# Starting the expert sum with a written-out first scatter instead of clearing its banks

## The chip, the cores and the metric

The kernel runs on one core of one Trainium2 chip, in float32. The metric is the device time of one execution in microseconds (us); lower is better.

## What is computed

The reference is two transformer blocks one after the other on 256 tokens of width 1024, with two layers each. Every layer is a token mixer followed by a hierarchical mixture of experts (MoE). The mixers are not touched by the change; the MoE is. Cut to what matters:

```python
def hier_moe(h, wg, bg, we, be, w1, w3, w2):
    ...
    g_sel = jnp.argmax(g_logits, axis=-1)                  # one group of 4
    top_l, top_i = lax.top_k(e_logits, TOP_K_EXPERTS)      # two of its 8 experts
    gates = g_gate[:, None] * jax.nn.softmax(top_l, axis=-1)
    ...
    def expert_block(args):
        xi, e = args
        hid = jax.nn.silu(xi @ w1[e]) * (xi @ w3[e])
        return hid @ w2[e]

    yb = lax.map(expert_block, (xb, blk_exp)).reshape(p_rows, d)
    y = jnp.zeros((t, d), h.dtype).at[buf_tok].add(yb * buf_w[:, None].astype(yb.dtype))
```

So `y`, 256 tokens by 1024, is a sum over 32 experts: each expert's results are scattered to its tokens, multiplied by the gate. The first block has experts of inner width 512, the second of 256. There are four such MoEs, called MoE 0 to MoE 3 here (`m` in the code; 0 and 1 have kind 1, 2 and 3 have kind 2).

## The kernel before, in words

Five engines run programs of their own, tied by counting semaphores. Each engine waits for a value that its `Engine` helper counts along (`q.due(name)`), and the producer raises it (`then_inc`). TensorE (PE) multiplies, VectorE (DVE) and ScalarE (ACT) read the products out of PSUM, SyncE (SP) starts all weight transfers. The order of the work on each engine is written out by hand; no scheduler changes it.

Weights come through a ring of `NR = 6` slots of 2048 KB. SP fills a slot as soon as PE has finished the product that used its old content (`unit_done`), so it runs at most six slots ahead of PE and no further. In an MoE of kind 1 a pair of experts takes all six slots, in one of kind 2 three.

PSUM has 8 banks of 128x512 float32. `y` takes banks 4 to 7, two of its eight 128x256 chunks in each bank. Since all scatters add into it over the whole MoE, `before` begins by clearing the four banks: `pe_clear` (L1859) multiplies a tile of zeros into a bank with `start=True`. At what points of the start of an MoE each bank is cleared is set by the table `CLEARS`, because the banks come free at different times: `at_once`, `turned` (when ScalarE has read the tokens that were turned into those banks), `ranked` (behind the products of the ranks) and `last` (behind the gather).

The start of an MoE runs so, with the lines as in the profile:

1. PE turns the router's logits (L632). DVE picks group and experts out of them in a row of small operations (`dve_route`, L1754 to L1789) and raises `route_done`. Meanwhile ScalarE turns the tokens into the tile `xN` (L678) and raises `tokens_ready`.
2. PE, meanwhile: the clears `at_once`, in MoE 2 and 3 also the rows of scales (L2260), three products that only keep it at work (`pe_warm`, L2246), the wait for `tokens_ready`, the clears `turned`, then `pe_ranks` (L1746, L1748, L1749), whose first product waits for `route_done`, then the clears `ranked`.
3. DVE makes the ranks (L1795), copies the counts (L1797) and compares ranks with slots (L1799, twice, `place_ready`). Then it works out where each expert's tokens start (L1802 to L1819), which later steps need.
4. PE gathers the tokens of the first pair of experts (`pe_gather`, L400), with the clears `last` behind it. ScalarE (L1970) and DVE (L1977) scale what was gathered (`xg_ready`).
5. `pe_experts`: pairs of experts. A pair (`pe_pair`) is the products up (L1924, in kind 2 L1932), half of the scatter of the pair before (L1908), the turn of the hidden tile (L1945), the other half of that scatter, the products down (L1956) and the turn of the gates (L1962). The first pair has no scatter and sorts the tokens instead. In kind 1 the first pair is written out and 15 more run in a hardware loop (`Fori`); in kind 2 two pairs are written out and 7 passes of two pairs run in the loop.

Of the kernel before, what the change touches and what calls it, by code (L numbers as in the profile page):

```python
# [19 lines left out]
P = 128  # L20
D = 1024
KD = D // P
# [194 lines left out]
def build(nc, a, vec_at, vec_w, dense_at, out):  # L217

    ctx = ExitStack()
    with ctx:  # L220
# [33 lines left out]
        def v(name, *dims):  # L254
            at, n = vec_at[name]
            return view(VEC + at, *(dims or (n,)))
# [23 lines left out]
        mm = nc.tensor.matmul  # L280
# [1471 lines left out]
        def dve_route(q, m, rbank):  # L1752
# [41 lines left out]
            q.e.wait_ge(sems["ranks_ready"], q.due("ranks_ready"))  # L1794
            V.tensor_tensor(rank, psum[:, rbank, 128:192].rearrange("p (t e) -> p t e", t=NT), chosen, ALU.mult).then_inc(sems["dve_step"], 1)  # L1795
            q.e.wait_ge(sems["dve_step"], q.due("dve_step"))
            V.tensor_copy(counts, psum[:, rbank, 192:224])  # L1797
            for t in range(NT):
                ins = V.tensor_tensor(place[:, t], along(rank[:, t, 0:2], CAP), over(v("slots"), 2), ALU.is_equal)  # L1799
            ins.then_inc(sems["place_ready"], 1)  # L1800
            q.e.wait_ge(sems["place_ready"], q.due("place_ready"))
            V.tensor_reduce(most, counts, AX.X, ALU.max)  # L1802
            V.tensor_tensor_scan(starts_f, ones[:, 0:E], counts, 0.0, ALU.mult, ALU.add).then_inc(sems["dve_step"], 1)
            q.e.wait_ge(sems["dve_step"], q.due("dve_step"))
# [48 lines left out]

        y = banks(4, 4, KD, S)

        def pe_clear(which):

            for b in which:
                mm(psum[:, b, :], v("zeros"), v("causal"), start=True, stop=False, skip_group_check=True)  # L1859


        def pe_gather(q):

            for k in range(KD):
# [37 lines left out]
            q.e.wait_ge(sems["sorted_even"], q.due("sorted_even", KD // 2))  # L1902
            q.e.wait_ge(sems["sorted_odd"], q.due("sorted_odd", KD // 2))

        def pe_scatter(q, first, last):

            for c in range(first, last):
                ins = mm(y[:, c, :], ysl[:, P * c:P * c + P], gatedT, start=False, stop=False, skip_group_check=True)  # L1908
            return ins

        def pe_pair(q, kind, first, sort):

            if not first:
                q.e.wait_ge(sems["xg_ready"], q.due("xg_ready", 2))
            if kind == 1:
                for n in range(2):
                    for part in range(2):
                        w = slot(q)
                        if n == 1 and part == 0 and not first:
                            q.e.wait_ge(sems["gatedT_ready"], q.due("gatedT_ready"))  # L1920
                        for i in range(KD // 2):
                            k = part * (KD // 2) + i
                            for e in range(2):
                                ins = mm(psum[CAP * e:CAP * e + CAP, n, :], xg[:, k, CAP * e:CAP * e + CAP],  # L1924
                                         sl(w, KD)[:, e * (KD // 2) + i, :], start=(k == 0), stop=(k == KD - 1),
                                         skip_group_check=True)
                        ins.then_inc(sems["unit_done"], 1)
            else:
                w = [slot(q), slot(q)]
                for k in range(KD):  # L1930
                    for e in range(2):
                        ins = mm(psum[CAP * e:CAP * e + CAP, 0, :], xg[:, k, CAP * e:CAP * e + CAP], sl(w[e], KD)[:, k, :],  # L1932
                                 start=(k == 0), stop=(k == KD - 1), skip_group_check=True)
                ins.then_inc(sems["unit_done"], 1)
                if not first:
                    q.e.wait_ge(sems["gatedT_ready"], q.due("gatedT_ready"))
            if not first:
                q.e.wait_ge(sems["results_ready"], q.due("results_ready", 2))
                pe_scatter(q, 0, KD // 2)
            if sort:  # L1940
                pe_sort(q)
            fc = 4 if kind == 1 else 2
            q.e.wait_ge(sems["hid_ready"], q.due("hid_ready"))
            for f in range(fc):
                ins = nc.tensor.transpose(psum[:, 0, P * f:P * f + P], hid[:, P * f:P * f + P], ident)  # L1945
            ins.then_inc(sems["hid_turned"], 1)
            if not first:
                pe_scatter(q, KD // 2, KD)
            q.e.wait_ge(sems["hidT_ready"], q.due("hidT_ready"))
            for half in range(2):  # L1950
                if kind == 1 or half == 0:
                    down = slot(q)
                for f in range(fc):
                    for e in range(2):
                        w = sl(down, KD)[:, 4 * e + f, :] if kind == 1 else sl(down, 4)[:, 2 * e + f, 512 * half:512 * half + 512]
                        ins = mm(psum[CAP * e:CAP * e + CAP, 2 + half, :], hidT[:, f, CAP * e:CAP * e + CAP], w,  # L1956
                                 start=(f == 0), stop=(f == fc - 1), skip_group_check=True)
                if kind == 1 or half == 1:
                    ins.then_inc(sems["unit_done"], 1)
            q.e.wait_ge(sems["gated_ready"], q.due("gated_ready"))  # L1960
            for t in range(NT):
                ins = nc.tensor.transpose(psum[:, 1, P * t:P * t + P], gated[:, t].rearrange("p a b -> p (a b)"), ident)  # L1962
            ins.then_inc(sems["gated_turned"], 1)
# [65 lines left out]
        def pe_experts(q, kind, passes):  # L2029
            n = PAIRS[kind]  # L2030
            per = {f"slot{(q.slot + j) % NR}": 16 for j in range(NR)}
            per.update(gatedT_ready=n, results_ready=2 * n, hid_ready=n, hidT_ready=n, xg_ready=2 * n, gated_ready=n)
            for g in range(n):
                pe_pair(q, kind, g == 0, g == 0)
            with nc.tensor.Fori(1, passes) as i:
                q.enter(i, per, 1)
                for g in range(n):
                    pe_pair(q, kind, False, False)
                q.leave(passes - 1)

        SUM_TURN = (0, 1, 2, 3)

# [202 lines left out]
            for _ in range(n):  # L2245
                mm(psum[:, bank, :], ident, view(VEC + vec_at["cum64"][0], 512), start=True, stop=True, skip_group_check=True)  # L2246

        CLEARS = (((6,), (4, 5), (), (7,)), ((5,), (6, 7), (), (4,)), ((), (4, 5), (6, 7), ()))

        def pe_moe(q, m, src, kind, rbank):  # L2250
            at_once, turned, ranked, last = CLEARS[min(m, 2)]
            if m < 2:
                q.skip("scale_ready")
            pe_clear(at_once)
            if m >= 2:
                q.e.wait_ge(sems["scale_ready"], q.due("scale_ready"))
                for n in range(2):
                    for t in range(NT):
                        col = spread[:, t, 0:1] if n == 0 else invs[:, t:t + 1]
                        ins = mm(psum[:, 1, S * n + P * t:S * n + P * t + P], col.broadcast_to([P, P]), ident, start=True, stop=True)  # L2260
                ins.then_inc(sems["rows_ready"], 1)
            pe_warm((1, 1, 3)[min(m, 2)], 3)
            q.e.wait_ge(sems["tokens_ready"], q.due("tokens_ready"))
            pe_clear(turned)
            pe_ranks(q, rbank)
            pe_clear(ranked)
            q.e.wait_ge(sems["place_ready"], q.due("place_ready"))
            pe_gather(q)
            pe_clear(last)
            q.e.wait_ge(sems["xg_ready"], q.due("xg_ready", 2))  # L2270
            pe_experts(q, kind, PASSES[kind])
            q.e.wait_ge(sems["starts_ready"], q.due("starts_ready"))
# [665 lines left out]
```

## Time and profile before

| | |
|---|---|
| Median of 3 runs | 2630.02 us (2628.97 to 2632.25) |
| The profiled execution | 2625.74 us |
| Its span on the core | 2624.1 us |
| TensorE busy | 2446.5 us, 93% of the span, 11516 matrix products |
| VectorE busy | 670.6 us, 26% |
| ScalarE busy | 449.8 us, 17% |
| HBM traffic | 769.56 MB, 293 GB/s over the span |
| Clears (L1859) | 32 records of 0.592 us (median) |
| Share of the chain that ended last | PE 70%, DMA 24%, DVE 3%, ACT 2% |

A float32 product shows as two records of TensorE, so `x2` in a row of the trace is one instruction of the program. Records of successive products overlap a little, since each holds its pipeline's latency; the distance from start to start tells what a product costs in a row of products. MoE 0 lies at 323 to 805 us, MoE 1 at 970 to 1457, MoE 2 at 1757 to 2030, MoE 3 at 2340 to 2615.

### The profile page before, as it was taken

Reading aid. Unit: us, or ns where it says so; the run is one execution under the profiler, and the core shown is the slowest. Engines: PE = TensorE matmul, PEld = TensorE weight load, DVE = VectorE, ACT = ScalarE, POOL = GpSimd, SP = SyncE. Lnnn points to the kernel's source line nnn. Section 1 sums busy time; section 2 is a strip of 40 time slices with the busy share of each in tenths; the row PEclk is TensorE's granted clock in tenths of the full one; section 3 lists DMA queues with packets and bytes.
Section 4 is the critical chain, followed back from the end, with each engine's and each line's share of the span. In section 5 each row is a group of like instructions: output and inputs, shape, how many; then the busy total and the mean of one; then the engine's idle time right before and its main releaser. Section 6 shows DMA issues by size and latency. Waiting matters only on the chain.

```text
span 2624.1 us, 28427 instructions
## 1 busy us (share of the span) xinstructions
PE 2446.5 (93%) x11516; PEld 1402.3 (53%) x11516; DVE 670.6 (26%) x1400; ACT 449.8 (17%) x814; POOL 0.2 (0%) x4
## 2 busy tenths in 40 slices
PE   7999999888889999988888998999999998999998
PEld 4775743333336673333333777874444777874443
DVE  2653321111003231101001532143112434042113
ACT  3141110000002121010000133011111242112111
POOL 0000000000000000000000000000000000000000
PEclk9999999999999999999999999999999999999999
DMA  9348669999997137999999542147999232148994
GB/s 401 131 183 366 253 275 428 429 428 429 428 428 289 66 129 330 429 428 429 429 428 429 208 147 106 67 192 281 428 423 376 97 129 97 64 193 333 427 421 179
DMA packets 53936, 769.56 MB, mean 293 GB/s; under 512 B 5984, under 2 KB 6496, under 8 KB 7008
## 3 DMA queue, kind: packets, MB, share of 16 engines
q1 hardware_dynamic: 53568, 768.17, 70.9%
q8 instruction: 57, 0.93, 0.1%
q10 hardware_dynamic: 288, 0.26, 0.0%
q14 instruction: 23, 0.19, 0.0%
HBM read 767.36 MB, written 1.05 MB: 293 GB/s over the span
## 4 chain that ended last, share of the span: by engine, by line
PE 70%; DMA 24%; DVE 3%; ACT 2%; issue 1%; SPq 0%; ACTq 0%; DVEq 0%
DMA slab<-in_experts 23%; PE psum L400 14%; PE psum L432 13%; PE psum L1932 9%; PE psum L1924 8%; PE psum L1956 7%; PE psum L1908 5%; PE psum L696 4%; PE psum L503 1%; DMA slab<-in_dense 1%; PE psum L1240 1%; PE psum L626 1%; PE psum L1962 1%; PE psum L1859 0%; PE psum L1945 0%
## 5 line engine op out<-in xcount | busy, mean ns | idle before, releaser
L1924 PE MATMUL psum<-slab 128*64 128x512 f32 x2048 | 462.0, 597 | 78.1 <-DMA slab<-in_experts 76.7
L400 PE MATMUL psum<-slab 128*128 128x256 f32 (+6 forms) x1560 | 388.3, 405 | 10.7 <-ACT slab L2443 7.0
L432 PE MATMUL psum<-slab 128*128 128x256 f32 x1504 | 343.3, 389 | 11.8 <-DVE slab L2733 6.6
L1956 PE MATMUL psum<-slab 128*64 128x512 f32 x1536 | 343.7, 597 | 2.6 <-ACT slab L1992 2.6
L1924 PEld LDWEIGHTS psum<-slab 128*64 128x64 f32 x2048 | 138.5, 137 | 380.1 <-issue 264.2
L400 PEld LDWEIGHTS psum<-slab 128*128 128x128 f32 (+2 forms) x1560 | 272.8, 188 | 120.3 <-issue 71.4
L432 PEld LDWEIGHTS psum<-slab 128*128 128x128 f32 x1504 | 292.9, 196 | 60.0 <-issue 8.8
L1908 PE MATMUL psum<-slab 128*128 128x256 f32 x1024 | 249.7, 385 | 3.0 <-DVE slab L2016 3.0
L1932 PE MATMUL psum<-slab 128*64 128x512 f32 x1024 | 226.8, 596 | 3.1 <-DVE slab L1977 3.1
L1908 PEld LDWEIGHTS psum<-slab 128*128 128x128 f32 x1024 | 183.3, 189 | 73.1 <-issue 48.7
L2004 DVE TENSOR_TENSOR slab<-psum,slab 128x512 f32<-128x512 f32 (+1 forms) x64 | 35.7, 558 | 707.6 <-PE psum L1924 509.5
L1956 PEld LDWEIGHTS psum<-slab 128*64 128x64 f32 x1536 | 104.7, 137 | 206.2 <-issue 202.6
L2014 DVE COPY slab<-psum 128x512 f32<-128x512 f32 x64 | 44.2, 691 | 427.8 <-PE psum L1956 427.8
L1932 PEld LDWEIGHTS psum<-slab 128*64 128x64 f32 x1024 | 70.7, 137 | 136.3 <-issue 132.9
L1988 ACT ACTIVATE slab<-psum 128x512 f32<-128x512 f32 (+1 forms) x64 | 31.4, 490 | 555.3 <-PE psum L1924 345.7
L696 PE MATMUL psum<-slab 128*128 128x256 f32 x512 | 114.8, 381 | 0.0
L696 PEld LDWEIGHTS psum<-slab 128*128 128x128 f32 x512 | 96.0, 190 | 16.9 <-issue 3.7
L1992 ACT ACTIVATE slab<-psum 128x512 f32<-128x512 f32 (+1 forms) x64 | 31.4, 490 | 389.7 <-PE psum L1945 389.7
L1996 ACT ACTIVATE slab<-psum 128x512 f32<-128x512 f32 x64 | 38.2, 597 | 251.8 <-PE psum L1956 251.8
L447 ACT ACTIVATE slab<-psum 128x512 f32<-128x512 f32 (+3 forms) x45 | 25.4, 565 | 244.1 <-PE psum L432 174.1
L2731 DVE TENSOR_TENSOR slab<-psum,slab 128x1024 f32<-128x1024 f32 x16 | 19.6, 1224 | 178.6 <-PE psum L400 178.6
L503 PE MATMUL psum<-slab 128*32 128x512 f32 x384 | 47.2, 615 | 7.3 <-DMA slab<-in_dense 4.9
(431 smaller groups left out, 1563.3 us busy)
## 6 DMA issues: line engine op xcount, KB each, us to landing
slab<-in_experts SPq DMA_DIRECT2D x288, 2048.0 KB, 20.1
slab<-in_dense SPq DMA_DIRECT2D x73, 2048.0 KB, 8.8
slab<-in_dense SPq DMA_DIRECT2D x2, 1680.0 KB, 18.5
slab<-in_vec SPq DMA_DIRECT2D x1, 2571.5 KB, 33.0
slab<-in_dense SPq DMA_DIRECT2D x1, 1328.0 KB, 27.6
slab<-in_dense SPq DMA_DIRECT2D x2, 640.0 KB, 14.4
slab<-in_xT SPq DMA_DIRECT2D x1, 1024.0 KB, 9.3
out<-slab SPq DMA_DIRECT2D x2, 512.0 KB, 2.6
```

The lines of the kernel that those rows point to most:

```text
L400: ins = mm(out_ap, lhs, rhs, start=(n == 0), stop=(n == len(pairs) - 1), skip_group_check=True)
L432: ins = mm(psum[:, b, S * j:S * j + S], narrow(s, width)[:, k, c0 + P * j:c0 + P * j + P], src[:, k, :], start=(k == 0), stop=(k == KD - 1 ...
L503: ins = mm(psum[32 * g:32 * g + 32, bank, :], silc[:, k:k + 1].broadcast_to([P, 32]), sl(s, KD)[:, k, :], start=(r == 0), stop=(r == KD // ...
L696: ins = mm(psum[:, b, S * j:S * j + S], sl(w[n // 2], KD)[:, k, c0:c0 + P], src[:, k, :], start=(part is early and j == 0 and k == early[0 ...
L1908: ins = mm(y[:, c, :], ysl[:, P * c:P * c + P], gatedT, start=False, stop=False, skip_group_check=True)
L1924: ins = mm(psum[CAP * e:CAP * e + CAP, n, :], xg[:, k, CAP * e:CAP * e + CAP], sl(w, KD)[:, e * (KD // 2) + i, :], start=(k == 0), stop=(k ...
L1932: ins = mm(psum[CAP * e:CAP * e + CAP, 0, :], xg[:, k, CAP * e:CAP * e + CAP], sl(w[e], KD)[:, k, :], start=(k == 0), stop=(k == KD - 1), ...
L1956: ins = mm(psum[CAP * e:CAP * e + CAP, 2 + half, :], hidT[:, f, CAP * e:CAP * e + CAP], w, start=(f == 0), stop=(f == fc - 1), skip_group_ ...
L1988: A.activation(sil[:, 0:f], psum[:, 0, 0:f], ACT.Silu).then_inc(sems["silu_ready"], 1)
L1996: A.activation(ysl[:, 0:512], psum[:, 2, :], ACT.Copy).then_inc(sems["results_ready"], 1)
L2004: V.tensor_tensor(hid[:, 0:f], up, sil[:, 0:f], ALU.mult).then_inc(sems["hid_ready"], 1)
L2014: V.tensor_copy(ysl[:, 512:], psum[:, 3, :]).then_inc(sems["results_ready"], 1)
```

## The change

The table `CLEARS` and `pe_clear` are gone, and with them 16 products of 128x512 with zeros, four in each MoE. The sum is begun by the first scatter instead: `pe_scatter` gets `begin`, and then its first product in each bank (even chunks) has `start=True`. For this the second pair has to be written out in kind 1 too, so that its scatter can differ from the ones in the loop, which now begins at pass 2 (`lead`). In MoE 0 and 1 `pe_warm` runs four products instead of three. On DVE the copy of the counts is moved behind the comparisons that PE waits for, and what reads the counts waits for the copy.

```diff
@@ dve_route
             V.tensor_tensor(rank, psum[:, rbank, 128:192]..., chosen, ALU.mult).then_inc(sems["dve_step"], 1)
             q.e.wait_ge(sems["dve_step"], q.due("dve_step"))
-            V.tensor_copy(counts, psum[:, rbank, 192:224])
             for t in range(NT):
                 ins = V.tensor_tensor(place[:, t], along(rank[:, t, 0:2], CAP), over(v("slots"), 2), ALU.is_equal)
             ins.then_inc(sems["place_ready"], 1)
-            q.e.wait_ge(sems["place_ready"], q.due("place_ready"))
+            V.tensor_copy(counts, psum[:, rbank, 192:224]).then_inc(sems["dve_step"], 1)
+            q.e.wait_ge(sems["dve_step"], q.due("dve_step"))
             V.tensor_reduce(most, counts, AX.X, ALU.max)
@@ pe_scatter, pe_pair
-        def pe_scatter(q, first, last):
+        def pe_scatter(q, first, last, begin=False):
             for c in range(first, last):
-                ins = mm(y[:, c, :], ysl[:, P * c:P * c + P], gatedT, start=False, stop=False, skip_group_check=True)
+                ins = mm(y[:, c, :], ysl[:, P * c:P * c + P], gatedT, start=begin and c % 2 == 0, stop=False, skip_group_check=True)
             return ins
-        def pe_pair(q, kind, first, sort):
+        def pe_pair(q, kind, first=False, sort=False, begin=False):
...
-                pe_scatter(q, 0, KD // 2)
+                pe_scatter(q, 0, KD // 2, begin)
...
-                pe_scatter(q, KD // 2, KD)
+                pe_scatter(q, KD // 2, KD, begin)
@@ pe_experts
-            for g in range(n):
-                pe_pair(q, kind, g == 0, g == 0)
-            with nc.tensor.Fori(1, passes) as i:
-                q.enter(i, per, 1)
+            lead = 2 // n
+            for g in range(2):
+                pe_pair(q, kind, g == 0, g == 0, g == 1)
+            with nc.tensor.Fori(lead, passes) as i:
+                q.enter(i, per, lead)
                 for g in range(n):
-                    pe_pair(q, kind, False, False)
-                q.leave(passes - 1)
+                    pe_pair(q, kind)
+                q.leave(passes - lead)
@@ pe_moe
-        CLEARS = (((6,), (4, 5), (), (7,)), ((5,), (6, 7), (), (4,)), ((), (4, 5), (6, 7), ()))
-            at_once, turned, ranked, last = CLEARS[min(m, 2)]
             if m < 2:
                 q.skip("scale_ready")
-            pe_clear(at_once)
-            if m >= 2:
+            else:
                 q.e.wait_ge(sems["scale_ready"], q.due("scale_ready"))
...
-            pe_warm((1, 1, 3)[min(m, 2)], 3)
+            pe_warm((1, 1, 3)[min(m, 2)], 4 if m < 2 else 3)
             q.e.wait_ge(sems["tokens_ready"], q.due("tokens_ready"))
-            pe_clear(turned)
             pe_ranks(q, rbank)
-            pe_clear(ranked)
             q.e.wait_ge(sems["place_ready"], q.due("place_ready"))
             pe_gather(q)
-            pe_clear(last)
```

Line numbers from L1802 to L1851 stay as they were; those behind fall by 5 to 12 (L1924 becomes L1918, L1932 L1926, L1908 L1902, L1956 L1950, L1977 L1971, L2246 L2241, L2260 L2251).

How the rows stand on TensorE at the start of MoE 0 and into its second pair, before (L1859 are the clears, L2246 the warming products, L1746 to L1749 the ranks, L400 with 128x128 the gather, L1924 and L1956 the products up and down):

```order
L632 MATMUL psum<-slab 128x36 x2
L1859 MATMUL psum<-slab 128x512
L2246 MATMUL psum<-slab 128x512 x3
L1859 MATMUL psum<-slab 128x512 x2
L1746 MATMUL psum<-slab 128x64
L1748 MATMUL psum<-slab 128x64
L1749 MATMUL psum<-slab 128x32
L400 MATMUL psum<-slab 128x128 x16
L1859 MATMUL psum<-slab 128x512
L1924 MATMUL psum<-slab 64x512 x32
```

And now, on the same engine and place, as far as the loop:

```order
L632 MATMUL psum<-slab 128x36 x2
L2241 MATMUL psum<-slab 128x512 x4
L1746 MATMUL psum<-slab 128x64
L1748 MATMUL psum<-slab 128x64
L1749 MATMUL psum<-slab 128x32
L400 MATMUL psum<-slab 128x128 x16
L1918 MATMUL psum<-slab 64x512 x32
...
L1918 MATMUL psum<-slab 64x512 x32
L1902 MATMUL psum<-slab 128x256 x4
L1939 MATMUL psum<-slab 128x128 x4
L1902 MATMUL psum<-slab 128x256 x4
L2030 UNCONDITIONAL_BRANCH
```

The warming products have taken the place of the first clear, nothing stands before the ranks or behind the gather, and the pair with the first scatter (L1902) stands ahead of the loop's branch.

TensorE at the start of MoE 2 (and 3), before:

```order
L2246 MATMUL psum<-slab 128x512 x3
L1859 MATMUL psum<-slab 128x512 x2
L1746 MATMUL psum<-slab 128x64
L1748 MATMUL psum<-slab 128x64
L1749 MATMUL psum<-slab 128x32
L1859 MATMUL psum<-slab 128x512 x2
L400 MATMUL psum<-slab 128x128 x16
```

And now:

```order
L2251 MATMUL psum<-slab 128x128 x4
L2241 MATMUL psum<-slab 128x512 x3
L1746 MATMUL psum<-slab 128x64
L1748 MATMUL psum<-slab 128x64
L1749 MATMUL psum<-slab 128x32
L400 MATMUL psum<-slab 128x128 x16
```

Two clears are gone ahead of the ranks and two ahead of the gather. On DVE, the comparisons (L1799, now L1798) and the copy of the counts (L1797, now L1800) have changed places:

```order
 L1795 TENSOR_TENSOR slab<-psum,slab 128x64
-L1797 COPY slab<-psum 128x32
-L1799 TENSOR_TENSOR slab<-slab 128x128 x2
+L1798 TENSOR_TENSOR slab<-slab 128x128 x2
+L1800 COPY slab<-psum 128x32
 L1802 TENSOR_REDUCE slab<-slab 128x1
```

## Rows read from the trace of the kernel before

**Rows 1.** Chain that ended last, by time (start, us, what), in MoE 0.

```profile
437.99 23.25 DMA slab<-in_experts
```

**Rows 2.** Timeline of PE, start of MoE 0: start, us, line, shapes, idle before.

```profile
323.17 1.12 PE L1859 MATMUL psum<-slab 128*128 128x512 f32 x2
324.13 2.74 PE L2246 MATMUL psum<-slab 128*128 128x512 f32 x6
326.70 1.88 PE L1859 MATMUL psum<-slab 128*128 128x512 f32 x4
328.42 0.33 PE L1746 MATMUL psum<-slab 128*128 128x64 f32 x2
...
330.11 3.84 PE L400 MATMUL psum<-slab 128*128 128x128 f32 x32 [0.94 <-DVE slab L1799]
333.79 1.03 PE L1859 MATMUL psum<-slab 128*128 128x512 f32 x2
335.49 1.94 PE L1924 MATMUL psum<-slab 128*64 128x512 f32 x8 [0.67 <-DVE slab L1977]
```

**Rows 3.** Timeline of DVE, start of MoE 0.

```profile
326.72 0.41 DVE L1789 SCALAR_TENSOR_TENSOR slab<-slab 128x32 f32<-128x32 f32 x2
...
329.21 0.22 DVE L1795 TENSOR_TENSOR slab<-psum,slab 128x64 f32<-128x64 f32 x1 [1.88 <-PE psum L1749]
329.47 0.19 DVE L1797 COPY slab<-psum 128x32 f32<-128x32 f32 x1
329.58 0.48 DVE L1799 TENSOR_TENSOR slab<-slab 128x128 f32<-128x128 f32 x2
...
331.92 0.26 DVE L1819 SCALAR_TENSOR_TENSOR slab<-slab 128x16 f32<-128x16 f32 x2
334.06 1.05 DVE L1977 TENSOR_SCALAR slab<-psum,slab 128x128 f32<-128x128 f32 x3 [1.88 <-PE psum L400]
```

**Rows 4.** Timeline of ACT, start of MoE 0: the tokens.

```profile
323.72 2.78 ACT L678 ACTIVATE slab<-psum,slab 128x512 f32<-128x512 f32 x4 [0.23 <-DVE slab L657]
```

**Rows 5.** Timeline of PE, start of MoE 2.

```profile
1761.85 1.88 PE L1859 MATMUL psum<-slab 128*128 128x512 f32 x4
1763.57 0.33 PE L1746 MATMUL psum<-slab 128*128 128x64 f32 x2
...
1765.96 3.73 PE L400 MATMUL psum<-slab 128*128 128x128 f32 x32
1771.22 4.08 PE L1932 MATMUL psum<-slab 128*64 128x512 f32 x18 [1.53 <-DVE slab L1977]
```

**Rows 6.** Timeline of DVE, start of MoE 2.

```profile
1761.26 0.42 DVE L1789 SCALAR_TENSOR_TENSOR slab<-slab 128x32 f32<-128x32 f32 x2
...
1764.36 0.23 DVE L1795 TENSOR_TENSOR slab<-psum,slab 128x64 f32<-128x64 f32 x1 [2.47 <-PE psum L1749]
...
1764.73 0.48 DVE L1799 TENSOR_TENSOR slab<-slab 128x128 f32<-128x128 f32 x2
```

**Rows 7.** Windows of MoE 0 and one later: us, engines' busy, PEclk, DMA share, GB/s.

```profile
335.00:340.00 5.00, 4.51 (x22) 1.64 (x24) 4.85 (x10) 0.01 (x1) 0.00 (x0) 1.00 0.00 0
...
360.00:370.00 10.00, 8.28 (x32) 3.05 (x32) 2.04 (x3) 2.57 (x4) 0.00 (x0) 1.00 0.08 30
...
2190.00:2193.00 3.00, 3.00 (x12) 2.62 (x11) 1.34 (x3) 1.45 (x1) 0.00 (x0) 0.50 0.00 0
```

**Rows 8.** Timeline of PE, MoE 2: second pair (written out), third and fourth (loop).

```profile
1798.14 7.09 PE L1932 MATMUL psum<-slab 128*64 128x512 f32 x32
...
1812.98 7.09 PE L1932 MATMUL psum<-slab 128*64 128x512 f32 x32
...
1827.83 2.37 PE L1932 MATMUL psum<-slab 128*64 128x512 f32 x10
```

**Rows 9.** Timeline of PE ahead of the third window of rows 7.

```profile
2187.29 0.63 PE L778 MATMUL psum<-slab 128*128 128x128 f32 x4 [1.00 <-DVE slab L768]
2189.44 1.88 PE L778 MATMUL psum<-slab 128*128 128x128 f32 x8 [1.51 <-DVE slab L768]
```

More of the change, by code:

```diff
@@ L1854, in build @@
         y = banks(4, 4, KD, S)
-        def pe_clear(which):
-            for b in which:
-                mm(psum[:, b, :], v("zeros"), v("causal"), start=True, stop=False, skip_group_check=True)
         def pe_gather(q):
```

## The prediction

> **What bounds the kernel now.** I read the chain that ended last first, because a change of four clears per MoE matters only where TensorE is on that chain. It is for 70% of the span. In MoE 0 the chain is TensorE's products for the first passes and turns into expert transfers at 437.99 us [rows 1]; MoE 1 does the same, while MoE 2 and 3 stay with TensorE. Next comes the timeline of TensorE and VectorE where the clears stand. The reader should see two things there. First, which clear has work behind it that was ready earlier: that one costs. Second, which clear is followed by idle time of TensorE: that one is free. Last come the windows, for the question whether time won at the start of an MoE survives in a stage that transfers bound.
>
> **MoE 0 (and 1).** Four clears in three places.
>
> - *The first* starts at 323.17 and takes 0.96 us to the next start; three warming products follow until 326.70 (2.57 us, 0.857 each) [rows 2]. Now four warming products start at 323.17: 0.96 for the first, as for whatever leads the row there, and 3 x 0.857 is 2.57, so they too end at 326.70. Cost and gain nil.
> - *The two before the ranks* run from 326.70 to 328.42, 1.72 us [rows 2]. The ranks need `tokens_ready` and `route_done`. ScalarE ends the tokens at 323.72 + 2.78 = 326.50 [rows 4], and VectorE raises `route_done` when L1789 ends, 326.72 + 0.41 = 327.13 [rows 3]. From such an end to TensorE's start the trace has 0.05 us: L1799 ends at 329.58 + 0.48 = 330.06 [rows 3] and the gather starts at 330.11 [rows 2]. So the ranks now start at 327.18, not 328.42: 1.24 us won, and the remaining 0.48 of the 1.72 goes into waiting for VectorE. What is late next is therefore the routing, not the tokens. Against that stands a start from idle: the gather takes 3.84 us after a pause [rows 2] and 3.73 right behind other products [rows 5], since its first weights can't load ahead. I charge the ranks 0.11 for it. The bounds are 0 and, from the 0.96 against 0.857 of the first product after a pause, the same 0.10 again, doubled for three small products: 0 to 0.2. Left: 1.13.
> - *The counts* leave the path: L1799 starts 0.11 us after L1797 does [rows 3], and takes its place. 0.11 won. The chain behind it on VectorE (L1802 to L1819) starts about 0.1 later against L1795. It ended at 331.92 + 0.26 = 332.18, while L1977, next on VectorE, waited for the gather until 334.06 [rows 3]: 1.88 us of cover, some 1.7 after the change. Nothing.
> - *The last clear* stands behind the gather, and TensorE then still idles 0.67 us for L1977 [rows 2]. Free before; its removal only makes that pause 1.54 us. Nothing.
>
> So the gather and all behind it start 1.24 us earlier. MoE 1 repeats these rows within 0.02 us (there are two of this pattern): 1.24 again.
>
> **MoE 2 (and 3).** Two clears before the ranks, two before the gather.
>
> - The warming products now hand over at 1761.85 [rows 5]. `route_done` comes at 1761.26 + 0.42 = 1761.68 [rows 6], 0.17 us before, so here TensorE is the later one and nearly all of 1763.57 - 1761.85 = 1.72 is won. The first weights of the ranks can load only from 1761.73 on, for which I charge 0.1 (0 to 0.2 as above). 1.62.
> - The gather started at 1765.96 because two more clears ran. `place_ready` came at 1764.73 + 0.48 = 1765.21 [rows 6], so it could have started at 1765.26: another 0.70. The counts add 0.11, and the gather starts from idle now, minus 0.11. Together 1.62 + 0.70 = 2.32 us. VectorE's chain (L1802 to L1819) moves with the ranks, 1.6 less 0.1 us earlier, the gather 2.3; its cover shrinks by some 0.8 us, of about as much as in MoE 0.
>
> MoE 3 repeats it: 2.32 again.
>
> **The second pair written out.** It has the same products in the same order; only `start` of four scatters differs, for which no row shows a price: products with and without it stand mixed in every accumulation. Code written out instead of looped: in MoE 2 the second pair is written out and takes 1812.98 - 1798.14 = 14.84 us, the third, in the loop, 14.85 [rows 8]. Nothing, with bounds of -0.1 and +0.5 for each of two.
>
> **Does the gain survive?** In MoE 0 transfers bind later. They would swallow the 1.24 us if their stream ran on from before the ranks. It doesn't: all six slots are full, the DMA share is 0.00 at 335 to 340, starts again when the first products free a slot, and is down to 0.08 at 360 to 370, because the sort frees none [rows 7]. Both restarts hang on TensorE, so the stream moves with it. Nothing outside that chain has a fixed time.
>
> **Sum.** 1.24 + 1.24 + 2.32 + 2.32 = 7.1 us, or 0.27%. Against the profiled execution: 2625.7 - 7.1 = 2618.6. The runs' median lies 4.3 above that execution, 2630.0, and I take the gain off that: **2622.9 us**. A difference of about 0.2%, 5.3 us, is what a measurement of this kernel can tell from none.
>
> **Rivals.**
>
> 1. *TensorE's clock falls at the new pauses, and the kernel gets slower.* Before, it doesn't at the starts of the MoEs: PEclk is 1.00 behind the pauses of 0.94 and 0.67 us in MoE 0 [rows 2, 7], and behind the 1.53 in MoE 2 the products up run 18 records in 4.08 us [rows 5], at the pace of later ones, 32 in 7.09 [rows 8]. Elsewhere it did fall: after pauses of 1.00 and 1.51 us with 0.63 of work between [rows 9] the next 3 us ran at 0.50, that is 1.2 GHz instead of 2.4 [rows 7], which cost about 1.5 us. The change leaves in MoE 2 a pause of about 0.9 before the gather and 1.53 behind it. For it: two pauses of the size of rows 9. Against: 3.7 us of work lie between them, not 0.63, and MoE 2 had its 1.53 already. One fall takes 1.5 to 1.7: one in all gives 2624.5, two 2626.1. It decides from five such stretches on: at all four MoEs and twice as long each, 4 x 3.2 = 12.8 us, it gives 2630.0 - 7.1 + 12.8 = 2635.7. The Trainium skill, TensorE: Matmul & The Clock Gate, Part 1, says that an idle array is set back to half clock and that only sustained work releases it; by that rule alone the pauses that the change opens are where to look, and the sum would be this rival's. The trace agrees that pauses come before falls, but so far not with pauses this far apart.
> 2. *Transfers swallow MoE 0 and 1.* Only 4.6 us would be left: 2625.4, no change by the bound. Rows 7 speak against it.
> 3. *The change doesn't free the ranks*, because something hidden behind the clears (bank readers, tokens) holds them. Then only 4 x 0.11 us come: 2629.6. Rows 3 and 4 speak against it; for MoE 2 the same order of the two releases.
> 4. *Luck elsewhere.* The clock also falls at places that the change doesn't touch. With all times shifted, a fall may come or go, 1.5 to 3.4 us either way. This is no case of its own but the width of mine.
>
> **How the numbers follow.** My forecast has 0.72, rival 1 0.14 (0.11 with one to three falls, 0.03 slower), rival 2 0.08, rival 3 0.06. The range runs from 7.1 + 3.4 won, 2619.5, to three short falls, 2628.0; rival 3 and the slow end of rival 1 stay outside. Faster: 0.68 of my 0.72 (the runs before spread by 3.3 us) and 0.04 of rival 1, 0.72. Slower: 0.03. The same: 0.25.
>
> **What the profile after would show.** Ranks 4.0 us behind the start of the warming products in MoE 0 (5.25 behind the first clear before) and right behind their end in MoE 2 (1.72); VectorE's wait for L1749 shorter by 1.1 and 1.6; the pause of TensorE before the products up at 1.5 in all four; PEclk 1.00 at all four starts; the loop passes as before. Wrong would be: a clock of 0.50 behind a gather, ranks that start later than `route_done` plus 0.05 to 0.1, or a MoE 0 that is longer from its ranks to its finish by what was won.

## The result and the profile after

| | before | changed |
|---|---|---|
| Median | 2629.49 us (6 runs, 2626.89 to 2632.25) | 2616.12 us (6 runs, 2615.14 to 2623.54) |
| Profiled execution | 2625.74 us | 2623.08 us |
| Its span, mean granted clock | 2624.1 us, 0.988 | 2621.4 us, 0.985 |
| TensorE | 2446.5 us, 11516 products | 2440.6 us, 11488 products |

The ratio is 0.995 with a 95% interval of 0.9939 to 0.996: 13.4 us faster where 7.1 were forecast, and 3.4 below the low end of my range. Beside it stands a puzzle: the two profiled executions differ by only 2.7 us. The changed kernel's six runs lie in two heaps, four at 2615 to 2617 and two at 2623 (the profiled one is of these). Further down the kernel before runs again beside each batch of experiments; one of its executions there took 3677 us at a clock of 0.651 and is left out of all means.

The starts of the MoEs came out close to the forecast. The row that each start is counted from, in the kernel before (MoE 0, then MoE 2):

```profile
322.92 0.32 PE L632 MATMUL psum<-slab 36*128 36x36 f32 x2 [0.47 <-ACT slab L671]
...
1757.46 0.31 PE L632 MATMUL psum<-slab 36*128 36x36 f32 x2 [0.47 <-ACT slab L671]
```

TensorE, changed kernel, start of MoE 0 (answers to [rows 2]):

```profile
322.70 0.31 PE L632 MATMUL psum<-slab 36*128 36x36 f32 x2 [0.47 <-ACT slab L671]
322.94 3.70 PE L2241 MATMUL psum<-slab 128*128 128x512 f32 x8
327.06 0.41 PE L1746 MATMUL psum<-slab 128*128 128x64 f32 x2 [0.42 <-DVE slab L1789]
...
328.73 3.84 PE L400 MATMUL psum<-slab 128*128 128x128 f32 x32 [0.84 <-DVE slab L1798]
334.10 1.08 PE L1918 MATMUL psum<-slab 128*64 128x512 f32 x4 [1.53 <-DVE slab L1971]
```

VectorE there (answers to [rows 3]):

```profile
326.50 0.42 DVE L1789 SCALAR_TENSOR_TENSOR slab<-slab 128x32 f32<-128x32 f32 x2
...
327.92 0.22 DVE L1795 TENSOR_TENSOR slab<-psum,slab 128x64 f32<-128x64 f32 x1 [0.81 <-PE psum L1749]
328.18 0.49 DVE L1798 TENSOR_TENSOR slab<-slab 128x128 f32<-128x128 f32 x2
...
330.63 0.26 DVE L1819 SCALAR_TENSOR_TENSOR slab<-slab 128x16 f32<-128x16 f32 x2
332.68 1.37 DVE L1971 TENSOR_SCALAR slab<-psum,slab 128x128 f32<-128x128 f32 x4 [1.78 <-PE psum L400]
```

TensorE, start of MoE 2 (answers to [rows 5]):

```profile
1759.24 0.31 PE L632 MATMUL psum<-slab 36*128 36x36 f32 x2 [0.47 <-ACT slab L671]
...
1761.05 2.74 PE L2241 MATMUL psum<-slab 128*128 128x512 f32 x6
1763.62 0.38 PE L1746 MATMUL psum<-slab 128*128 128x64 f32 x2
...
1765.26 3.84 PE L400 MATMUL psum<-slab 128*128 128x128 f32 x32 [0.84 <-DVE slab L1798]
1770.63 3.65 PE L1926 MATMUL psum<-slab 128*64 128x512 f32 x16 [1.53 <-DVE slab L1971]
```

To see here: in MoE 0 the ranks wait for L1789 and nothing else, in MoE 2 they follow right on the warming products; the gather waits 0.84 us for L1798 in both; VectorE's chain ends at 330.89 and leaves 1.78 us until L1971. I call the distance from L632 to the first product up "the start". It was 12.57, 12.56, 13.76 and 13.76 us in the four MoEs and is 11.40, 11.40, 11.39 and 11.41 us. Won: 1.17 + 1.16 + 2.37 + 2.35 = 7.05 us.

So 6 us of the 13 come from elsewhere. The clock of TensorE (PEclk, the granted share of 2.4 GHz; 0.50 is 1.2 GHz, and a stretch at 0.50 is called a fall below) is the suspect, since the two heaps differ in it: the runs at 2615 to 2617 us had a mean clock of 0.988 to 0.989, those at 2623 of 0.985 to 0.986. To put a price on it, I summed (1 - PEclk) x TensorE's busy time over windows of 2 us up to 2608 us (a fall at the very end of the span costs at most 1 us more); called "lost to the clock" below. It is 22.1 us in the profiled execution of before and 27.2 in that of the changed kernel. Span less this: 2602.0 and 2594.2 us, 7.8 apart. In the two profiles the clock hid 5 us of the gain. In the runs it must have added 6, if nothing else did.

### The profile page after: what moved, and what is told of

It reads as the page before. It is cut to its first block, busy times and chain, and to the rows that moved or that the text cites. A ratio compares the mean times of both kernels' runs of the same rounds, so it can differ in the third digit from the quotient of the medians.

```text
span 2621.4 us, 28363 instructions
## 1 busy us (share of the span) xinstructions
PE 2440.6 (93%) x11488; PEld 1399.5 (53%) x11488; DVE 670.5 (26%) x1400; ACT 450.1 (17%) x814; POOL 0.2 (0%) x4
## 4 chain that ended last, share of the span: by engine, by line
PE 70%; DMA 24%; DVE 4%; ACT 2%; issue 1%; SPq 0%; ACTq 0%; DVEq 0%
DMA slab<-in_experts 23%; PE psum L400 14%; PE psum L432 13%; PE psum L1926 9%; PE psum L1918 8%; PE psum L1950 7%; PE psum L1902 5%; PE psum L696 4%; PE psum L503 1%; DMA slab<-in_dense 1%; PE psum L1240 1%; PE psum L1956 1%; PE psum L626 0%; PE psum L1939 0%; PE psum L746 0%
## 5 line engine op out<-in xcount | busy, mean ns | idle before, releaser
L1918 PE MATMUL psum<-slab 128*64 128x512 f32 x2048 | 461.9, 597 | 80.3 <-DMA slab<-in_experts 77.2
L400 PE MATMUL psum<-slab 128*128 128x256 f32 (+6 forms) x1560 | 389.1, 406 | 12.2 <-ACT slab L2431 7.0
L432 PE MATMUL psum<-slab 128*128 128x256 f32 x1504 | 344.9, 391 | 11.8 <-DVE slab L2721 6.6
L1950 PE MATMUL psum<-slab 128*64 128x512 f32 x1536 | 343.7, 596 | 2.6 <-ACT slab L1986 2.6
L1918 PEld LDWEIGHTS psum<-slab 128*64 128x64 f32 x2048 | 138.4, 136 | 381.1 <-issue 264.1
L400 PEld LDWEIGHTS psum<-slab 128*128 128x128 f32 (+2 forms) x1560 | 272.9, 188 | 121.5 <-issue 70.6
L432 PEld LDWEIGHTS psum<-slab 128*128 128x128 f32 x1504 | 293.9, 196 | 60.7 <-issue 8.9
L1902 PE MATMUL psum<-slab 128*128 128x256 f32 x1024 | 249.6, 385 | 3.0 <-DVE slab L2010 3.0
L1926 PE MATMUL psum<-slab 128*64 128x512 f32 x1024 | 226.8, 595 | 3.1 <-DVE slab L1971 3.1
L1902 PEld LDWEIGHTS psum<-slab 128*128 128x128 f32 x1024 | 183.1, 189 | 73.3 <-issue 48.7
L1950 PEld LDWEIGHTS psum<-slab 128*64 128x64 f32 x1536 | 104.6, 137 | 206.3 <-issue 202.7
L1926 PEld LDWEIGHTS psum<-slab 128*64 128x64 f32 x1024 | 70.7, 137 | 136.4 <-issue 133.0
## 6 DMA issues: line engine op xcount, KB each, us to landing
slab<-in_dense SPq DMA_DIRECT2D x2, 640.0 KB, 14.8
```

What stands on the lines that cost most here:

```text
L400: ins = mm(out_ap, lhs, rhs, start=(n == 0), stop=(n == len(pairs) - 1), skip_group_check=True)
L432: ins = mm(psum[:, b, S * j:S * j + S], narrow(s, width)[:, k, c0 + P * j:c0 + P * j + P], src[:, k, :], start=(k == 0), stop=(k == KD - 1 ...
```

## The experiments

Three theories were set against each other. **A1**: the starts win 7.05 us, and the number of falls of the clock hangs on how the places where it can fall lie to each other in time, which the change moved. **A0**: falls are chance, independent of the kernel. **A2**: products of zeros, or the written-out pair, do something else. (The expectations of the first four runs say A for A1 and B for "the missing 6 us are a gain in some other stage".) The kernel before ran beside each batch, 11 to 29 times.

### Both kernels again

No edit.

> The changed kernel once more, for a second trace of it. Theory A (the change wins 7.05 us at the starts of the four MoEs, as its trace shows, and the other 6 of the 13 come from the half clock falling more rarely in these runs): the four starts, from L632 to the first product up, measure 11.4 us each again; the time from run to run varies with the granted clock, so that span less the time lost to the clock (span x (1 - clock)) is the same within 2 us in every run. Theory B (the change saves some 6 us elsewhere too, in the expert loops or transfers): a stage outside the starts is shorter than before by more than 1 us in this trace as well.

> The kernel before once more. Theory A: its span less the time lost to the clock is constant from run to run as well, and lies 7 us above that of the changed kernel; its times lie between 2625 and 2633 us with the number of falls of the clock. Theory B: the corrected times differ by 13 us.

Measured: changed 2617.32 us (2610.99 to 2624.03, 6 runs), ratio 0.9947 (0.9931 to 0.9963); before 2632.93 (12 runs, 2626.99 to 2633.4), beside it 2631.86 (23 runs), ratio 1.0002 (0.9992 to 1.0012). Starts of 11.40 to 11.41 and of 12.57, 12.56, 13.76, 13.76 us. Lost to the clock 17.6 and 29.5 us, span less this 2592.5 and 2599.95. Together with the first pair the means are 2593.4 and 2601.0, 7.6 apart: A1 and A0, not B. All runs together say the same, more roughly: span times mean clock is 2584.2 us as a mean over the 12 runs of the changed kernel and 2590.6 over 60 of before, 6.4 apart. From run to run of one batch it varies by 2.7 to 4.4 us, more than the 2 expected; rounding the clock to three digits alone makes up to 2.6 of it.

The two heaps did not come back: these six runs lie at 2611, 2612, 2617, 2618, 2621 and 2624 us. Chance is hard to hold, though: over three batches before has a mean of 2630.6 us (66 runs; clock 0.985 in the 60 that list it) and the changed kernel one of 2617.7 (12 runs, 0.988).

### The parts of the change

`peel_only` keeps all clears and writes out the second pair, whose scatter starts the banks:

```diff
-            for g in range(n):
-                pe_pair(q, kind, g == 0, g == 0)
-            with nc.tensor.Fori(1, passes) as i:
+            lead = 2 // n
+            for g in range(2):
+                pe_pair(q, kind, g == 0, g == 0, g == 1)
+            with nc.tensor.Fori(lead, passes) as i:
```

> The kernel before with the second pair written out and the sum begun by its scatter, all clears left in place. Theory A: nothing at the starts (12.6, 12.6, 13.8 and 13.8 us, as before), loop passes as before; corrected time as before within 1 us, measured time as before within 2 us. Theory B: if the written-out pair or the start flag saves the 6 us, this kernel is at about 2623 us with the same starts.

Measured: 2630.26 us (12 runs), ratio 0.9993 (0.9985 to 1.0002); starts as before, MoE stages as before; lost to the clock 26.1, span less this 2599.9. The written-out pair and the start flag show no cost and no gain beyond the noise of some 2 us. They don't hold the missing 6 us.

`after_old_counts` puts the copy of the counts back:

```diff
+            V.tensor_copy(counts, psum[:, rbank, 192:224])
             for t in range(NT):
                 ins = V.tensor_tensor(place[:, t], ...)
             ins.then_inc(sems["place_ready"], 1)
-            V.tensor_copy(counts, psum[:, rbank, 192:224]).then_inc(sems["dve_step"], 1)
-            q.e.wait_ge(sems["dve_step"], q.due("dve_step"))
+            q.e.wait_ge(sems["place_ready"], q.due("place_ready"))
```

> The changed kernel with the copy of the counts put back ahead of the comparisons. Both theories: each start is 0.11 us longer, 11.5 us, 0.44 in all, which the times can't tell; the trace can. Theory A: the time is one of the two levels that the changed kernel showed, about 2616 or 2623 us.

Measured: 2620.85 us (6 runs), starts of 11.50, 11.51 and 11.51 us in MoE 1 to 3: the counts are worth 0.1 each. MoE 0 took 13.13, and that is my rival 1 caught in the act. Windows of that kernel around its gather:

```profile
320.00:327.00 7.00, 5.61 (x20) 2.62 (x18) 5.33 (x33) 5.54 (x13) 0.00 (x0) 1.00 0.60 254
327.00:331.00 4.00, 3.56 (x17) 3.56 (x18) 2.26 (x14) 0.29 (x2) 0.00 (x0) 0.57 0.03 6
331.00:338.00 7.00, 5.47 (x35) 2.99 (x36) 4.89 (x10) 2.79 (x5) 0.00 (x0) 1.00 0.00 0
```

And its gather in TensorE's timeline:

```profile
327.44 5.47 PE L400 MATMUL psum<-slab 128*128 128x128 f32 x32 [0.94 <-DVE slab L1799]
```

PEclk (the column behind the POOL one) is 0.57, mostly 1.2 GHz, and the gather takes 5.47 us instead of 3.84. It happened in one of the 56 starts without clears that all traces of this study hold, and cost 1.6 us.

`moe01_only` clears as before in MoE 2 and 3. `moe23_only` clears in MoE 0 and 1 and has the copy of the counts where it was before. The edit of the first:

```diff
+            if m >= 2:                      # moe01_only
+                pe_clear((4, 5))
             pe_ranks(q, rbank)
+            if m >= 2:
+                pe_clear((6, 7))
```

> The clears are gone in MoE 0 and 1 only; in MoE 2 and 3 two stand ahead of the ranks and two behind, as before. Theory A1 (the starts win 7.05 us, and how often the clock falls depends on how the places where it can fall lie in time to each other, which the change moved): starts of 11.4, 11.4, 13.7 and 13.7 us, and without the clock's losses 2597.7 us of span; if the distance from the mixer at 1460 to the one at 2030 is what counts, falls are as frequent as before, so about 2629 us. Theory A2 (the falls became fewer because TensorE's work at the start of an MoE is another, without products of zeros): also frequent falls for the part of MoE 2 and 3, about 2626 us. Theory A0 (falls come at random, the 13 us were luck): 2629.5 - 2.3 = 2627 us as a mean over both days.

> The clears are gone in MoE 2 and 3 only, the counts stand ahead of the comparisons. Starts of 12.6, 12.6, 11.5 and 11.5 us, 4.5 us less than before, and without the clock's losses 2595.5 us of span. Theory A1: the mixers of MoE 2 and 3 lie to each other as in the changed kernel, so its rarer falls come back: 2619 to 2621 us. Theory A0: 2631.5 - 4.5 = 2627 us.

Measured: `moe01_only` 2629.25 us (11 runs), ratio 0.9997 (0.9988 to 1.0006), mean clock 0.986, starts 11.40, 11.40, 13.75, 13.76; `moe23_only` 2620.37 us (12 runs), ratio 0.9975 (0.9962 to 0.9988), mean clock 0.987, starts 12.56, 12.56, 11.50, 11.50. Spans less the clock's losses were 2600.2 and 2594.2 (forecast 2597.7 and 2595.5, so this measure is good to 2 or 3 us). Clears gone in MoE 0 and 1 alone bring nothing that can be told from noise: 0.5 us in the mean, though 2.3 are won at the starts. Those gone in MoE 2 and 3 bring 7.3 us in the mean (0.9975; the runs lie between 2615 and 2633), of which 4.5 are won at the starts. The two gains add up to 8 us and not to 13, so the parts don't simply add, and the clock gave back some 3 of its 6 us. A2 had 2626 for the first. A1 fits in kind, with the placing of MoE 2 and 3 as the greater part, but that the distance between the mixers at 1460 and 2030 us alone counts is not shown.

### Nothing but delay in MoE 2

If distance is the cause, plain delay must do it. `late_by_k` is the changed kernel with k more warming products ahead of the ranks of MoE 2 (0.857 us each), `before_late_by_1` the same on the kernel before:

```diff
-            pe_warm((1, 1, 3)[min(m, 2)], 4 if m < 2 else 3)
+            pe_warm((1, 1, 3)[min(m, 2)], (4, 4, 3 + k, 3)[m])
```

> The changed kernel with two more warming products in MoE 2, ahead of its ranks: 2 x 0.857 = 1.7 us of nothing but delay, on the path. Theory A0 and A2: 2617.3 + 1.7 = 2619 us, with the mean clock of the changed kernel (0.988). Theory A1: the clock's losses change, by several us either way, so the time differs from 2619 by more than 2 us.

> The same with four more warming products, 3.4 us. Theory A0 and A2: 2617.3 + 3.4 = 2620.7 us. Theory A1: if the placing counts and repeats, this delay may have the falls of the undelayed kernel again and also lie at 2620 to 2621, while the delay of 1.7 us doesn't fit a line between.

> The kernel before with one more warming product in MoE 2, 0.86 us of delay and nothing else. MoE 2 then starts its products up 3.2 us later than in the changed kernel, close to the delay of late_by_4, whose mean clock was the changed kernel's. Theory A1 (the placing of the mixers to each other decides how often the clock falls): the frequent falls go, and although there is more work the kernel is some 5 us faster than before, about 2625 us, with a mean clock of 0.987 to 0.988. Theory A0 and A2: 2630.5 + 0.9 = 2631 us, mean clock 0.985.

> The changed kernel with three more warming products in MoE 2: its start is then 11.4 + 2.57 = 14.0 us, close to the 13.8 of the kernel before, with no clear in it. Theory A1: the frequent falls of before come back, mean clock 0.985 to 0.986, 2617.5 + 2.6 + 4 to 6 = 2624 to 2626 us, slower than with the longer delay of late_by_4 (2620). Theory A2 (the clears themselves make falls): mean clock 0.988, 2620 us.

> One more warming product in MoE 2, a start of 12.3 us. Theory A1: between the changed kernel (0.988) and late_by_2 (0.987), so 2617.5 + 0.9 + 0 to 2 = 2618 to 2621 us. Theory A0: 2618.4 us.

| kernel | start of MoE 2, us | runs | median, us | mean, us | mean less the delay | same, below the before beside it | mean clock |
|---|---|---|---|---|---|---|---|
| changed (two batches) | 11.4 | 12 | 2616.9 | 2617.7 | 2617.7 | 12.9 | 0.988 |
| late_by_1 | 12.2 | 6 | 2620.3 | 2621.0 | 2620.2 | 11.3 | 0.987 |
| late_by_2 | 13.1 | 7 | 2622.6 | 2622.5 | 2620.8 | 8.7 | 0.987 |
| late_by_3 | 13.9 | 12 | 2625.1 | 2625.9 | 2623.3 | 8.1 | 0.986 |
| late_by_4 | 14.8 | 5 | 2619.9 | 2620.3 | 2616.9 | 12.7 | 0.988 |
| before | 13.8 | 66 | - | 2630.6 | 2630.6 | 0 | 0.985 |
| before_late_by_1 | 14.6 | 11 | 2627.9 | 2628.0 | 2627.1 | 3.9 | 0.987 |

The rows come from several batches, and the mean of before beside them lay between 2629.5 and 2631.5 us; the column "same, below the before beside it" takes this out. Read down it: with the same work everywhere else the gain shrinks from 12.9 to 8.1 us as the start of MoE 2 comes near 13.9 and is back at 14.8. Three products of delay cost more than four: 5.5 us below before against 9.2, uncertain by 1.7. The intervals of their ratios, 0.9981 (0.997 to 0.9992) and 0.9965 (0.9953 to 0.9978), still touch. The stronger case is the kernel before, made to work 0.86 us longer: it got faster, ratio 0.9988 (0.9979 to 0.9997), 3.1 us in the mean, uncertain by 0.7. I had expected 5 us there and a clock of 0.987 to 0.988; it was 3 to 4 and 0.9865. A0 and A2 had 2631 us for it and fail there. A2 also fails on `late_by_3`, where it had 2620 us and a clock of 0.988: there is no clear in it, and it has 2625.9 and 0.986. With 5 to 12 runs a row, whose means are uncertain by 0.4 to 1.5 us, the shape of the curve between is not settled.

Where it happens is seen in windows at the start of the last mixer and at its end, the columns as in [rows 7]. The kernel before:

```profile
2020.00:2085.00 65.00, 59.33 (x269) 48.81 (x266) 40.51 (x91) 12.76 (x22) 0.00 (x0) 0.89 0.29 108
2180.00:2245.00 65.00, 57.32 (x251) 47.78 (x250) 22.95 (x21) 15.09 (x32) 0.00 (x0) 0.92 0.18 65
```

The changed kernel's slow-clocked profile (2623 us):

```profile
2020.00:2085.00 65.00, 59.33 (x267) 49.17 (x268) 40.48 (x91) 12.76 (x22) 0.00 (x0) 0.89 0.29 106
2180.00:2245.00 65.00, 57.32 (x251) 47.76 (x250) 22.40 (x21) 15.10 (x32) 0.00 (x0) 0.92 0.19 65
```

The changed kernel again (`a_again`, 2612 us):

```profile
2020.00:2085.00 65.00, 60.08 (x277) 47.95 (x276) 40.18 (x93) 15.40 (x25) 0.00 (x0) 0.95 0.34 122
2180.00:2245.00 65.00, 58.33 (x269) 49.47 (x268) 15.94 (x14) 12.39 (x22) 0.00 (x0) 0.97 0.27 98
```

`late_by_4`:

```profile
2020.00:2085.00 65.00, 59.33 (x286) 46.94 (x285) 39.93 (x90) 13.53 (x24) 0.00 (x0) 0.95 0.40 153
2180.00:2245.00 65.00, 57.33 (x273) 48.07 (x272) 25.72 (x23) 15.10 (x32) 0.00 (x0) 0.97 0.18 65
```

The last mixer, from the last scatter of MoE 2 to L632 of MoE 3, took 314 to 315 us in the traces of `before`, `b_again`, `moe01_only`, `late_by_2`, `after_old_counts` and the first of the changed kernel, 310 to 311 in `peel_only`, `before_late_by_1`, `late_by_1` and `late_by_3`, and 307 in `a_again`, `moe23_only` and `late_by_4`. These 7 us are of the size of the distance between the two heaps, and more than half of the 11 us between the two traces of the changed kernel. It also shows that one trace is one draw: `late_by_3` was profiled at 2619.1 us, its lowest run.

### Filling the pauses

If pauses of TensorE bring the falls, warming products in them should take falls away without delaying anything. Four kernels fill pauses of the changed one: `fill_finish` sets two products ahead of the scale rows at the end of each MoE (a pause of 2.27 us) and two behind them in MoE 2; `fill_both` adds two where I took the pause of 3.31 us in the mixers to be; `fill_merge` has three at another such place, `fill_all` that and `fill_finish`.

```diff
+            pe_warm(5, 2)                              # fill_finish
             q.e.wait_ge(sems["scale_ready"], q.due("scale_ready"))
...
             ins.then_inc(sems["rows_ready"], 1)
+            if m == 2:
+                pe_warm(5, 2)
...
+            q.e.wait_ge(sems["gate_read"], q.due("gate_read"))      # fill_both, behind both halves of the merge
+            pe_warm(4, 2)
...
+                        pe_warm(4, 3)                  # fill_merge, in pe_out ahead of the wait for mix_ready
                     q.e.wait_ge(sems["mix_ready"], q.due("mix_ready"))
```

> The changed kernel with two warming products in the pause of 2.27 us ahead of the scale rows at the end of each MoE, and two more behind them in MoE 2, where 2.30 us of pause follow. They fill pauses and delay nothing. If pauses of TensorE make the clock fall at the starts of the mixers (810, 1456 and 2032 us in the traces: 1.5, 2.8 and 2.9 us lost), these falls go: no fall there in the trace, 3 to 6 us faster than the changed kernel, 2612 to 2615 us, unless later places then fall more often. If the clock falls for another reason: 2617.5 us with the same falls.

> As fill_finish, with two more warming products in the pause of 3.31 us ahead of the late part of the mixers' output product (2230 us in the trace, 3.0 us lost each time it fell). If pauses are the cause: that fall goes too, and one of its neighbours at 1650; 1 to 3 us below fill_finish, about 2611 us. Otherwise the same as fill_finish.

> The changed kernel with three warming products between the early and the late part of the mixers' output product (m 2 and 3), where TensorE pauses 3.31 us for VectorE's last sum; 2.6 us of it are filled. If the pause makes the clock fall there: no fall at 1650 and 2230 in the trace (2.9 us lost in each so far), and 2 to 5 us faster than the changed kernel, unless falls move elsewhere as in fill_finish. If not: the falls stay, 2617.5 us.

> fill_merge and fill_finish in one. If pauses make the clock fall: no falls at the five filled places, clock 0.989 or more, some 2612 us. If the falls only move: 2617 to 2620 us.

Measured: `fill_finish` 2619.81 us (5 runs), clock 0.988. The falls at 810, 1456 and 2032 us are gone in its trace, but there are others, at 1011 and 1489, and the one at 2066 has stayed; nothing won. `fill_both` 2624.71 (9 runs), `fill_merge` 2627.84 (11) and `fill_all` 2624.22 (11), with clocks of 0.989, 0.985 and 0.989: misses of my own. The pause of 3.31 us stood in their traces unchanged, and the new products stood where TensorE was busy; in `fill_merge`, TensorE, second mixer:

```profile
2307.32 20.96 PE L700 MATMUL psum<-slab 128*128 128x256 f32 x96
2328.12 2.74 PE L2245 MATMUL psum<-slab 128*128 128x512 f32 x6
2330.69 1.90 PE L700 MATMUL psum<-slab 128*128 128x256 f32 x8
```

No pause ahead of L2245: 2.57 us of delay in each mixer. The pause at 2230 ends with L432, the features of the merge's second half, so the products belong ahead of that half:

```diff
                 if half == 1:
                     u = Units(q)
+                    q.e.wait_ge(sems["gate_read"], q.due("gate_read"))
+                    pe_warm(4, 3)
+                    q.skip("gate_read")
                     q.e.wait_ge(sems["gts_read"], q.due("gts_read", 4))
...
-                q.skip("gate_read", 2)
+                if half == 1:
+                    q.skip("gate_read", 2)
```

> The changed kernel with three warming products ahead of the second half of the mixer's merge, inside TensorE's pause of 3.31 us. The pause in the trace shrinks to about 0.6 us and nothing is delayed. If the pause makes the clock fall: no fall at 1650 and 2230 us (2.9 us lost in each when it fell), mean clock 0.989 and about 2613 us. If falls only move to other places: 2617 us with clock 0.988.

> fill_half with two warming products ahead of the scale rows at the end of each MoE as well. If pauses make the clock fall: none at 810, 1456, 1650 and 2230 either, mean clock 0.990, about 2611 us; if they only move, 2617 to 2620 us.

TensorE in the changed kernel, then in `fill_half`:

```profile
2213.48 14.14 PE L400 MATMUL psum<-slab 128*128 128x256 f32 x64 [0.93 <-ACT slab L2431]
2230.93 5.49 PE L432 MATMUL psum<-slab 128*128 128x256 f32 x12 [3.31 <-DVE slab L2721]
```

```profile
2205.21 14.14 PE L400 MATMUL psum<-slab 128*128 128x256 f32 x64 [0.93 <-ACT slab L2431]
2219.19 2.74 PE L2241 MATMUL psum<-slab 128*128 128x512 f32 x6
2222.68 9.58 PE L432 MATMUL psum<-slab 128*128 128x256 f32 x43 [0.75 <-DVE slab L2725]
```

The pause is 0.75 us now, and nothing is delayed: from the start of L400 to that of L432 it is 17.45 us in the first and 17.47 in the second. `fill_half` has no fall at 1650 or 2220 in its trace and runs in **2613.56 us** (6 runs, 2611.25 to 2616.29), ratio to before 0.9937 (0.9925 to 0.9949), mean clock 0.990. That is 3 to 4 us below the changed kernel in medians and means (2613.6 against 2617.7), the fastest kernel of the study. Its interval overlaps with the changed kernel's, so by how much it is faster is not settled. One trace without those falls proves little, since `a_again` has none there either. All traces together say more: in the 34 pauses of 3.31 us of the other 17 traces the clock fell 23 times, in or behind the four pauses of 0.75 us never. With `fill_finish`'s first part added (`fill_half_finish`) it is 2617.67 us (6 runs, clock 0.990), no better: falls at 1650 and 2230 are gone there too, but the one at 813, which that filler was to take away, is still there, as in `fill_all` at 809, and there are ones at 1014 and 2066. Why it is slower than `fill_half` at the same mean clock is open.

## Why the prediction was wrong

- **Cover, clears, ranks, gather, counts: right.** Forecast 1.24, 1.24, 2.32, 2.32; measured 1.17, 1.16, 2.37, 2.35. In MoE 0 the ranks started 4.12 us behind the start of the warming products, not 4.0: L1789 ended at 326.92 and they began at 327.06, 0.14 behind it instead of 0.05. The chain from L1789's end to L1795's start took 1.00 us (0.95 forecast). The pause ahead of the products up is 1.53 in all four, as said.
- **The second pair written out: right as far as can be told.** `peel_only` shows nothing above its noise of 2 us.
- **Survival in the transfer-bound MoEs: right as far as can be told.** From the first product up to the last scatter MoE 0 and 1 take 469 to 471 us in the four traces of the two kernels.
- **Rival 1 (falls at the new pauses): right in kind, rare in fact.** One start of 56, 1.6 us. (Rows 7 cover only what lies behind the pause of 0.67 us; behind the one of 0.94, at 330 to 334 us, the trace of before has a PEclk of 1.00 too.)
- **The failed step is rival 4, "a fall may come or go, 1.5 to 3.4 us either way. This is no case of its own but the width of mine."** I took the falls as chance with mean zero. They are chance in one execution, but how often they come hangs on the kernel's timing: before lost much in nearly every run (clock 0.985), and one product of plain delay in MoE 2 gave back 3.9 us of it. The term was 0 +- 3.4 and measured some 6 us of gain: 12.9 us between the means less 7.05 at the starts. Why the new placing brings fewer falls than the old one is open; the runs show only that the placing matters. A sign of it stood in the times shown: the profiled execution of before, 2625.7, lay 4.3 below the median and below all three runs. I carried the 4.3 us over as a constant offset and didn't ask what made it.
- The forecast direction was right, for the 7 us that I could read off. The other 6 came with it without my having foreseen them: that is luck.

## What to carry to other kernels

Price a change by the distance between two instructions on either side of it, and compare that with the trace after; here it was right to 0.1 us while the total was off by 6. Where a time differs from the sum by more, look at the mean clock of every run before looking for a mechanism, and give the kernel a plain delay at the same place: if a delay makes the kernel faster, or a shorter one costs more than a longer one, the kernel's timing, not its work, is speaking. Compare each kernel with runs of before from its own batch: here these differed by 2 us. Fill the pauses that come ahead of falls, but check in the trace that the filler stands inside the pause and that the falls haven't moved on.

## What was not expected of the hardware

- Delay alone changed the mean time by some 4 us beyond its own length: one product more made the kernel before 3.1 us faster, and `late_by_3` is 3.7 us slower than `late_by_4`, each against the kernel before beside it (uncertain by 0.7 and 1.7). It came with how often TensorE ran at 1.2 GHz.
- The clock also falls where TensorE has no pause. In the kernel before, TensorE's rows follow each other without a gap from 2033.65 us on, and in the middle of this one the clock goes from 1.00 to 0.50:

```profile
2057.36 12.19 PE L400 MATMUL psum<-slab 128*128 128x256 f32 x64
```

```profile
2064.00:2065.00 1.00, 1.00 (x8) 0.59 (x6) 0.96 (x3) 0.38 (x2) 0.00 (x0) 1.00 0.00 0
...
2068.00:2069.00 1.00, 1.00 (x7) 1.00 (x6) 0.96 (x3) 0.00 (x0) 0.00 (x0) 0.50 0.00 0
```

That one cost 3.4 us. Falls with no pause of TensorE over 0.4 us in the 8 us before them stand in 17 of the 19 traces, at 2065 to 2073 us or, one mixer earlier, at 1488 to 1500, and cost 1.7 or 3.4 us each. What brings them is open; no experiment touched it.
